# Down product as three products of split operands, scatters with a bounds check and a value projection that starts at the first tile, in a two-layer convolution, attention and mixture-of-experts trunk

## The reference

```
scores = sigmoid(xt @ router_w)                    # 64 experts, the 8 best of each token
h = silu(xb @ w_gate[e]) * (xb @ w_up[e])          # xb: an expert's tokens, up to 128 a block; 1024 -> 256
y = h @ w_down[e]                                  # 256 -> 1024, times the token's gate
routed[token] += y                                 # over the 8 experts of each token
out = routed + shared expert
```

## Time and profile before

| | us |
|---|---|
| median of the 3 runs (lowest, highest) | 2486.3 (2479.9, 2489.4) |
| the profiled execution, its own time | 2482.5 |
| its span, first to last instruction | 2480.7 |
| TensorE busy | 2296.2 |
| VectorE busy | 1606.8 |
| ScalarE busy | 1076.4 |
| GpSimd busy | 684.8 |

### The profile page before, as it was taken

One profiled execution on the slowest core, in us unless ns is written; L12 is line 12 of the kernel. 1 busy time (PEld: TensorE's weight loads), 2 busy tenths in 40 slices (PEclk: granted clock), 3 DMA queues, 4 the chain that ended last, 5 costly groups with the idle time before them and its releaser, 6 DMA issues.

```text
span 2480.7 us, 32934 instructions
## 1 busy us (share of the span) xinstructions
PE 2296.2 (93%) x9437; PEld 1633.7 (66%) x9437; DVE 1606.8 (65%) x1737; ACT 1076.4 (43%) x1215; POOL 684.8 (28%) x698
## 2 busy tenths in 40 slices
PE   7948889999999999869999999798999999999994
PEld 4413557767666667559988888554667777676673
DVE  4874557777767667552377787436677777776675
ACT  3651135555555555422243333112555555555552
POOL 3970213443434333200000000002233433334331
PEclk9969889999999999979999999889999999999997
DMA  6210359999999999633322222132999999999994
GB/s 216 68 34 0 127 202 346 371 366 375 360 350 362 365 345 372 209 134 93 94 77 69 79 83 83 56 119 70 339 366 367 368 364 363 367 372 355 360 364 142
DMA packets 197117, 592.57 MB, mean 239 GB/s; under 512 B 26605, under 2 KB 96277, under 8 KB 161732
## 3 DMA queue, kind: packets, MB, share of 16 engines
q1 hardware_dynamic: 165140, 517.92, 56.0%
q0 software_dynamic: 31920, 73.91, 12.2%
HBM read 579.16 MB, written 51.38 MB: 254 GB/s over the span
## 4 chain that ended last, share of the span: by engine, by line
PE 81%; DVE 6%; DMA 4%; ACT 1%; issue 1%; POOLq 0%; SPq 0%; DVEq 0%; ACTq 0%
PE PS L1355 29%; PE PS L1376 18%; PE PS L1464 11%; PE PS L1448 5%; PE PS L1246 5%; PE PS L1342 5%; DMA W<-in_exp_w_down 4%; PE PS L1280 2%; PE PS L1477 1%; PE PS L1364 1%; PE PS L1502 1%; PE PS L1326 1%; DMA acc<-BIG,IDXS 1%; PE PS L1299 1%; PE PS L1489 1%
## 5 line engine op out<-in xcount | busy, mean ns | idle before, releaser
L998 DVE TENSOR_TENSOR WL<-W,WH 128x2048 fp32r<-128x2048 f32 x276 | 621.3, 2293 | 197.3 <-ACT WH L679 185.9
L679 ACT ACTIVATE WH<-W 128x2048 fp32r<-128x2048 f32 x276 | 512.4, 1907 | 43.1 <-DVE IDX L976 42.4
L1376 PE MATMUL PS<-W,BIG 128*128 128x512 f32 x1104 | 498.6, 594 | 11.1 <-issue 5.0
L1355 PE MATMUL PS<-WH,XH 128*128 128x512 f32 x1104 | 446.6, 405 | 8.8 <-DVE XL L991 8.8
L1355 PE MATMUL PS<-WH,XL 128*128 128x512 f32 x1104 | 435.2, 394 | 0.0
L1355 PE MATMUL PS<-WL,XH 128*128 128x512 f32 x1104 | 432.6, 392 | 0.0
L589 POOL DMA_INDIRECT acc<-BIG,IDXS x138 | 259.1, 1878 | 471.3 <-issue 371.3
L1376 PEld LDWEIGHTS PS<-W,BIG 128*128 128x128 f32 x1104 | 199.2, 190 | 212.8 <-issue 205.1
L1355 PEld LDWEIGHTS PS<-WH,XH 128*128 128x128 f32 x1104 | 209.7, 190 | 48.2 <-DVE XL L991 9.6
L689 ACT ACTIVATE BIG<-PS 128x512 f32<-128x512 f32 x138 | 82.5, 598 | 362.5 <-PE PS L1376 362.5
L1355 PEld LDWEIGHTS PS<-WH,XL 128*128 128x128 f32 x1104 | 209.2, 189 | 46.0
(11 more groups left out here) (233 smaller groups left out, 3110.2 us busy)
## 6 DMA issues: line engine op xcount, KB each, us to landing
W<-in_exp_w_gate SPq DMA_DIRECT2D x138, 1024.0 KB
W<-in_exp_w_up SPq DMA_DIRECT2D x138, 1024.0 KB
W<-in_exp_w_down SPq DMA_DIRECT2D x138, 1024.0 KB
RAW<-in_w_kv SPq DMA_DIRECT2D x48, 512.0 KB, 3.8
RAW<-in_attn_w_q SPq DMA_DIRECT2D x24, 512.0 KB, 3.7
W<-in_conv_w_in SPq DMA_DIRECT2D x8, 1024.0 KB, 11.4
acc<-BIG SPq DMA_DIRECT2D x9, 512.0 KB, 3.7
W<-in_conv_w_out SPq DMA_DIRECT2D x4, 1024.0 KB, 6.5
```

Source lines behind the costliest of these rows:

```text
L679: A(WH[:, s, c, :], W[:, 3 - 3 * s + c, :], ACT.Copy).then_inc(s_wh[l], 1)
L998: v.tensor_tensor(WL[s][:, c, :], W[:, 3 - 3 * s + c, :], WH[:, s, c, :].bitcast(F32), ALU.subtract).then_inc(s_wl[l], 1)
L1355: last = mm(PS[:, 3 + s, :].rearrange("p (a b) -> p a b", a=2), a, w, start=(k == 0 and i == 0), stop=(k == KT - 1 and i == 2))
L1376: last = mm(PS[:, 5 + h, :], HTm[:, s, k * P:(k + 1) * P], wd[:, k, h * 512:(h + 1) * 512], start=(k == 0), stop=(k == 1))
```

## The change

The down product becomes a split product like gate/up's. ScalarE copies the down weights to a high part `WDH` and the transposed hidden to `HTH`; VectorE subtracts to get `WDL` and `HTL`; TensorE sums three products, 12 matmuls of 512 columns in float32r. Both halves of the output are now copied by ScalarE. The loads of gate and up wait for a count of low parts that now has the down parts in it; the load of down waits as before. The scatter has a bounds check at row 511, and the spare rows of `acc`, with the store of zeros to them at the start, are gone. Gathers stay four blocks ahead. Between the layers, three pieces of `w_kv` are split ahead of the norm instead of two behind it, and the V product of the first three pieces runs tile by tile as the tiles come; only from the fourth piece on it runs over all tiles. The next norm's vectors are loaded behind piece 9 instead of piece 3. Left out of the diff are hunks that only merge the semaphores `s_pj` and `s_tb` of the two layers into one each.

```diff
--- before.py
+++ after.py
@@ -45,7 +45,7 @@
     xrows = nc.dram_tensor("xrows", [T, D], F32, kind="Internal").ap()
-    acc = nc.dram_tensor("acc", [T + P, D], F32, kind="Internal").ap()
+    acc = nc.dram_tensor("acc", [T, D], F32, kind="Internal").ap()
     etab = nc.dram_tensor("etab", [2, OVER], I32, kind="Internal").ap()
@@ -130,6 +130,13 @@
+        _, WDH1, HTL, _, HTH, WDH0, _, WDL = lay_out([("to_WDH1", [8192 + 10240], F32), ("WDH1", [2, D], F32R), ("HTL", [2, F], F32R),
+                                                      ("to_HTH", [20736 - 12800], F32), ("HTH", [2, F], F32R),
+                                                      ("WDH0", [2, D], F32R), ("to_WDL", [256], F32),
+                                                      ("WDL", [SLOTS, CH], F32R)])
+        WDH = (WDH0, WDH1)
+
+
         _, XTH, _, RAW, PH, PL, XTL = lay_out([("to_XTH", [NT, D], F32), ("XTH", [KT, T], F32R), ("to_RAW", [23552], F32),
@@ -184,10 +191,9 @@
         Hm = big(20224, 2, F)
-        HTm = big(20736, 2, F)
-
-
-        s_vec, s_posd, s_zero = sem("vec_loaded"), sem("pos_loaded"), sem("zeros_stored")
+
+
+        s_vec, s_posd = sem("vec_loaded"), sem("pos_loaded")
         s_xin = [sem(f"x_loaded{n}") for n in range(NT)]
@@ -238,10 +244,10 @@
         s_ht = [sem(f"hidden_transposed{i}") for i in range(2)]
-        s_he = [sem(f"hidden_T_copied{i}") for i in range(2)]
+        s_hh = [sem(f"hidden_T_high{i}") for i in range(2)]
+        s_he = [sem(f"hidden_T_low{i}") for i in range(2)]
         s_yd = [sem(f"expert_out{i}") for i in range(2)]
-        s_ya = [sem(f"expert_out_low_copied{i}") for i in range(2)]
-        s_yv = [sem(f"expert_out_high_copied{i}") for i in range(2)]
+        s_ya = [sem(f"expert_out_copied{i}") for i in range(2)]
         s_scat = [sem(f"scattered{i}") for i in range(2)]
@@ -389,7 +395,7 @@
                     for c in range(2):
-                        sp.wait_ge(s_wl[l], b * 2 - 3 + c)
+                        sp.wait_ge(s_wl[l], 1 + c if isinstance(b, int) and b == 2 else b * 3 - 6 + c)
                         load(3 - 3 * s + c, e)
@@ -429,8 +435,6 @@
                 sp.dma_start(RB[:, l, :], router_bias[l:l + 1, :].broadcast_to([P, E])).then_inc(s_rw, 16)
-            sp.wait_ge(s_cst, 1)
-            sp.dma_start(acc[T:T + P, :], XG[:, 0, :]).then_inc(s_zero, 16)
             for i in range(6, n_first):
@@ -438,7 +442,7 @@
             for j, src in enumerate(pieces):
-                if j == PIECES:
+                if j == 3 * PIECES:
                     ln_vectors(2)
@@ -462,7 +466,6 @@
             sp.wait_ge(s_out, 16 * NT)
-            sp.wait_ge(s_zero, 16)
@@ -474,7 +477,6 @@
-            pool.memset(XG[:, 0, :], 0.0)
             pool.memset(ones[:, :], 1.0)
@@ -524,7 +526,6 @@
                 pool.wait_ge(s_norm, 2 * NT * l + NT)
-                pool.wait_ge(s_zero, 16)
                 link(pool.memset(XG[:, 0:2, :], 0.0))
@@ -579,15 +580,14 @@
                     pool.wait_ge(s_ic[l], copies)
-                    pool.wait_ge(s_ya[l], b + 1)
-                    pool.wait_ge(s_yv[l], b + 1)
+                    pool.wait_ge(s_ya[l], b * 2 + 2)
                     if not (isinstance(b, int) and b == 0):
 ...
                         pool.indirect_dma_start(acc, bass.IndirectOffsetOnAxis(IDXS[0:r, s:s + 1], axis=0), YB[0:r, s, :],
-                                                None, compute_op=ALU.add).then_inc(s_scat[l], 16)
+                                                None, bounds_check=T - 1, oob_is_err=False, compute_op=ALU.add).then_inc(s_scat[l], 16)
@@ -678,24 +678,40 @@
+                def down_high(b, s, it):
+                    act.wait_ge(s_mw[l][5 - 3 * s], it * 16 + 16)
+                    if not (isinstance(b, int) and b < 2):
+                        act.wait_ge(s_yd[l], b - 1)
+                    A(WDH[s].rearrange("p k n -> p (k n)"), W[:, 5 - 3 * s, :], ACT.Copy).then_inc(s_wh[l], 1)
+
+                def hidden_high(b, s):
+                    act.wait_ge(s_ht[l], b + 1)
+                    if not (isinstance(b, int) and b < 2):
+                        act.wait_ge(s_yd[l], b - 1)
+                    A(HTH[:, s, :], PS[:, 2, 0:F], ACT.Copy).then_inc(s_hh[l], 1)
+
                 def silu(b, s):
 ...
-                def out_low(b, s):
+                def out(b, s):
                     act.wait_ge(s_yd[l], b + 1)
 ...
                         act.wait_ge(s_scat[l], (b - 1) * 16)
-                    A(YB[:, s, 0:512], PS[:, 5, :], ACT.Copy).then_inc(s_ya[l], 1)
+                    for h in range(2):
+                        A(YB[:, s, h * 512:(h + 1) * 512], PS[:, 5 + h, :], ACT.Copy).then_inc(s_ya[l], 1)
                 def step(b, s, it, more):
+                    hidden_high(b, s)
                     if more:
 ...
                         rows_high(b + 2, s)
-                    out_low(b, s)
+                    if more or s == 0:
+                        down_high(b + 1, 1 - s, it + s)
+                    out(b, s)
@@ -714,13 +730,16 @@
                 rows_high(1, 1)
+                down_high(0, 0, 0)
+                for k in range(2):
+                    act.wait_ge(s_acc[l][k], 16 * NT // 2)
                 step(0, 0, 0, True)
 ...
                     step(it * 2 + 1, 1, it, True)
-                step(n * 2 - 2, 0, None, False)
-                step(n * 2 - 1, 1, None, False)
+                step(n * 2 - 2, 0, n - 1, False)
+                step(n * 2 - 1, 1, n - 1, False)
@@ -767,7 +786,6 @@
             moe(0)
-            norm_round(1)
@@ -778,10 +796,12 @@
-            for j in range(PIECES - 1):
+            for j in range(PIECES):
                 piece_high(j)
+            norm_round(1)
             for j in range(n_v):
-                piece_high(j + PIECES - 1)
+                if j >= 1:
+                    piece_high(j + PIECES - 1)
                 if j % 4 == 3:
@@ -994,7 +1014,7 @@
                     for c in range(2):
-                        dve.wait_ge(s_wh[l], b * 2 + 1 + c)
+                        dve.wait_ge(s_wh[l], b * 2 + 1 + c if isinstance(b, int) and b < 2 else b * 3 + c)
                         v.tensor_tensor(WL[s][:, c, :], W[:, 3 - 3 * s + c, :], WH[:, s, c, :].bitcast(F32),
@@ -1005,25 +1025,25 @@
-                def hidden_T(b, s):
-                    dve.wait_ge(s_ht[l], b + 1)
-                    v.tensor_copy(HTm[:, s, :], PS[:, 2, 0:F]).then_inc(s_he[l], 1)
-
-                def out_high(b, s):
-                    dve.wait_ge(s_yd[l], b + 1)
-                    if not (isinstance(b, int) and b < 2):
-                        dve.wait_ge(s_scat[l], (b - 1) * 16)
-                    v.tensor_copy(YB[:, s, 512:D], PS[:, 6, :]).then_inc(s_yv[l], 1)
+                def down_low(b, s, copies):
+                    dve.wait_ge(s_wh[l], copies)
+                    v.tensor_tensor(WDL[:, 5 - 3 * s, :], W[:, 5 - 3 * s, :],
+                                    WDH[s].rearrange("p k n -> p (k n)").bitcast(F32), ALU.subtract).then_inc(s_wl[l], 1)
+
+                def hidden_low(b, s):
+                    dve.wait_ge(s_hh[l], b + 1)
+                    v.tensor_tensor(HTL[:, s, :], PS[:, 2, 0:F], HTH[:, s, :].bitcast(F32), ALU.subtract).then_inc(s_he[l], 1)
                 def step(b, s, more):
-                    hidden_T(b, s)
+                    hidden_low(b, s)
                     if more:
 ...
                         rows_low(b + 2, s)
-                    out_high(b, s)
+                    if more or s == 0:
+                        down_low(b + 1, 1 - s, b * 3 + 8 if more else n * 6)
@@ -1035,6 +1055,7 @@
                 rows_low(1, 1)
+                down_low(0, 0, 5)
                 step(0, 0, True)
@@ -1118,10 +1138,12 @@
-            for j in range(PIECES - 1):
+            for j in range(PIECES):
                 piece_low(j)
+            norm_round(1)
             for j in range(n_v):
-                piece_low(j + PIECES - 1)
+                if j >= 1:
+                    piece_low(j + PIECES - 1)
                 if j % 4 == 3:
@@ -1345,7 +1367,7 @@
                     pe.wait_ge(s_xl[l], b + 1)
-                    pe.wait_ge(s_wl[l], b * 2 + 2)
+                    pe.wait_ge(s_wl[l], b * 2 + 2 if isinstance(b, int) and b < 2 else b * 3 + 1)
                     if not (isinstance(b, int) and b < 2):
@@ -1364,17 +1386,19 @@
-                def down_proj(b, s, it):
+                def down_proj(b, s, splits):
                     pe.wait_ge(s_he[l], b + 1)
-                    pe.wait_ge(s_mw[l][5 - 3 * s], it * 16 + 16)
+                    pe.wait_ge(s_wl[l], splits)
                     if not (isinstance(b, int) and b == 0):
-                        pe.wait_ge(s_ya[l], b)
-                        pe.wait_ge(s_yv[l], b)
-                    wd = W[:, 5 - 3 * s, :].rearrange("p (k n) -> p k n", k=2)
+                        pe.wait_ge(s_ya[l], b * 2)
+                    wdl = WDL[:, 5 - 3 * s, :].rearrange("p (k n) -> p k n", k=2)
```

(59 more changed lines are left out.)

2 lines of the change are left out of this document (1 added, 1 removed).

## The result

The changed kernel takes **2569.31 us** (median of 4 runs, 2565.21 to 2571.77); the kernel before took 2484.99 in the same rounds. The ratio is 1.0339, 95% interval [1.0321, 1.0357]: slower by 84 us, outside the predicted range. The profiled execution has a span of 2566.1 us, 85.4 more than before.

A forecast was written before the change was run, and what follows sets the result against it. It took TensorE's program and the full DMA engines as joint bounds; 5 + 3 - 5 = +3 us on the profiled 2482.5 gave 2485.5, and 2489 us as the median. The range was 2445 to 2535 us.

The forecast's parts named there:

- the slower rival: Expert blocks: down weights land late, ScalarE's copy waits in front of its program; 10.4 us per block, 2525 us, chance 0.16.
- the new order on ScalarE: Expert blocks: next block's down copy stands ahead of output and later copies; two-block loop, 10.15 us per block, +5 us.
- Landing to issue, 10.3: Two-block loop: from down weights' landing through ScalarE's and VectorE's copies and SyncE's issues to next down issue, 10.3 us.
- The landing, 9.6: Two-block loop: down transfer from issue to landing, 2.5 + 9.8 - 2.7 = 9.6 us.
- The spread, 0.2: Expert blocks: allowance for uneven scatters, twice today's 0.11 us, added to 9.95 us per block.
- TensorE's idle time: Expert blocks: the 0.7 us saved on TensorE goes into waiting for VectorE's low copies; 0.6 to 0.9 us idle per block.
- Faster, DMA-bound at 9.8: Expert blocks: less queued DMA serves transfers quicker, blocks of 9.8 to 9.85 us, -38 us, 2446 us; chance 0.34.
- Scatters: Expert blocks: scatters wait for each other, GpSimd slowed by VectorE subtractions; loop grows 0.3 us, +40 us, 2529; chance 0.09.
- No saving: Scatters: bounds check leaves padded rows' cost, DMA time stays 10.07, block 10.3 us, 2510 us; chance 0.06.
- the signs named: Expert blocks: signs of being right, with blocks 10.1 to 10.2 us apart; 9.8 or below, or above 10.3, meant wrong.
- The V product: Value projection between layers: tile-by-tile start beside a norm about 11 us later, -5 us, between -13 and +5.
- The start and end of the stages, +3: Each expert stage: copies ahead of the first step and one more serial hop at the end, +1.5 us per layer.

The follow-up runs named there:

- e6: Changed kernel with SyncE loading the down weights' expert number ahead of its waits for the gate and up slots: 2569.49 us, ratio 1.0331.
- e11: Changed kernel with the up loads behind the first ones bringing only half their bytes: 2460.57 us (one run).
- e4: Changed kernel with SyncE issuing the down load ahead of gate and up instead of behind them: 2487.74 us, ratio 1.0036.
- e2: Kernel before with the scatters' bounds check alone: 2481.3 us, ratio 0.9991.
- e1: Kernel before with the split down product alone, no bounds check, V product as before: 2584.55 us, ratio 1.0415.
- e10: Changed kernel with loads in the order down, gate, up and both expert numbers loaded ahead of the waits: 2502.79 us, ratio 1.0075.
- e12: Changed kernel with the down weights' high and low copies moved into their own block's step and loads ordered down, gate, up: 2545.59 us (one run).
- e3: Changed kernel with down weights loaded only for the first two blocks of a layer: 2418.2 us (one run).

## Why the prediction was wrong

*The mechanism was one of its rivals, mispriced.* The late landing was there as the slower rival, 2525 us at a chance of 0.16. The step that failed is the sum of **the new order on ScalarE**: 10.3 (landing to next issue) + 9.6 (landing), with 0.2 of spread, 10.15 us per block. The trace has 10.8 + 11.2 in the chain (mean of 43 landings), 11.0 per block where the loop holds, and 10.82 on average: 0.67 us per block more, 132 times, 88 us (+5 was said for the blocks, +93.5 came); the other terms took some 6 us off again.

- *Landing to issue, 10.3, was 10.8.* I let down's issue follow the low copies by 0.5 us. It also has up's issue ahead of it and the load of its own expert number (the row of L402 and what surrounds it): up is issued at 1969.02, down at 1970.28, 1.26 behind. The steps were all in the trace of before; the number's load was not counted. The copies ahead of it came 0.3 us shorter than summed (up's issue 9.5 us behind the landing, 9.8 said), which hides a part of that miss. e6 shows that this term alone could be had back without any gain.
- *The landing, 9.6, was the larger error.* I took it as the mean work of the queue, 9.8 us a block from gate's issue on plus 2.5. Gate's issue to down's landing was to be 12.3 and is 14.1 in the median: two of the three loads and the rows stand ahead of down, and it has landed only when the slowest of the 16 engines has (the first is done 7.4 us behind the issue, the last 10.5, medians). e11 shows which way this depends: half a megabyte less ahead of it, 1.9 us sooner. e6 shows the other side: an issue 0.6 us sooner, nothing. So the form, a drain of what is queued from gate's issue on, had the right direction and was 1.8 us too small. A landing of fixed length behind its own issue, my first reading of the result, was wrong. How the 1.8 us divide between the spread of the engines and dearer bytes stays open.
- *The spread, 0.2, has no measure of its own.* The chain's landings run from 9.4 to 13.7 us; it is part of the difference between the median 10.5 and the chain's mean of 11.2.
- *A term that was not there: the clock.* TensorE's idle time was forecast, 0.6 to 0.9 us per block, and taken as harmless. The slow gate/up products behind it are 18 us of the chain, up to a fifth of the 93.5; their cause is still the late landing, as e4 has 5 of them and not 18. What the time would be with the waits and the full clock, no run shows.
- *The rival's own sum.* (10.3 + 10.5) / 2 is 10.4 without the 0.2 of spread that the forecast adds. With it the rival is 10.6, about +65 us, some 2550, outside the stated range.
- *The other rivals.* "Faster, DMA-bound at 9.8" had the wrong floor. It rests on the time that the skipped rows save, and in e2 the weights' queue took 14 of the 35 us back; the 368 GB/s beside it is the figure of one window. Over 400 to 1000 and 1850 to 2400 us the kernel before moves 363 and 364 GB/s at a share of 1.01, e2 358 and 359 at 1.00 and 1.01, e4 358 and 357 at 0.99 and 0.98. So with the bounds check the engines stayed as full and moved 1% less, and no run with all the weights has blocks below the 10.11 us of the kernel before. The Trainium skill (DMA: Bandwidth & Descriptors, Specifications) gives about 358 GB/s as the HBM limit and 368 derated; over these stretches the kernel before lies between the two, and e2 and e4 at the first. Whether a version without any loop would get below 10.2 no run shows; in e4 the last load of the three, now up, is again in the chain. "Scatters" is out as first cause, by e1 and e4: GpSimd waits less for an earlier scatter than before, 354 us against 390.7, though stretches of the chain run through them (4% of the span), and in e10 and e12 they hold 15%. The contention that the Trainium skill names (GPSIMD Engine Reference, Key points) does not set the pace here: in e4 the gathers' index copy takes 1152 ns in the mean, in the changed kernel 882, and e4 is 82 us faster. Only in e3, with 1821 ns, does GpSimd hold much of the chain. "No saving" is out for the second queue, with 67.18 MB and 10.5% as worked out, but not for the blocks: e2 shows the engines as full as before.
- *What held.* The split product takes 2.76 us per block (2.74 to 3.0 said; the row of L1401 at 2078.78 above).

ScalarE waiting for the landing before its new copy, the share just under 1 and 0.6 to 0.9 us of idle TensorE per block (7.9 in 100 us, 0.85) were the signs named; all three came, and so did the 67 MB of the second queue. They fit the slower rival as well, so they told nothing of which was right; what did tell was the distance of the blocks, 10.8 us, above the 10.3 named as a sign of being wrong. The V product came near in number, and in part by luck: the norm starts 14.1 us behind the last scatter's landing (3.4 before), 10.7 later where 11 was said, the first V product stands inside it, and the stage from the last block on takes 1259.71 - 1077.98 = 181.7 us against 187.2, -5.5 for a predicted -5. Of these, 3.6 lie between the last scatter's landing and the end of the V product (162.9 us against 166.5); the other 1.9 lie ahead of that landing, where the forecast had put 0 to +4.

```profile
1094.31 2.46 DMA acc<-BIG,IDXS
...
1110.88 1.29 DVE bns L904 x2
...
1122.20 5.98 PE PS L1463 x18
...
1259.71 0.46 PE PS L1502 x2
```

The start and end of the stages, +3, came as about 0 at the start and the end of the execution and as these -1.9 between the layers. The stretch between V product and layer 1 is 2.7 us shorter, for which the forecast had no term and I have no cause: 93.5 - 5.5 - 2.7 = 85.3 of the span's 85.4.

## What to carry to other kernels

A copy that moves ahead of other work on an in-order engine turns a hidden transfer into a loop: then count, from the trace, every issue and register load up to the next issue, and price the landing as the drain of everything queued before it, until the slowest engine is done, not as its bytes and a latency. Give the last place in the queue to the load that is needed last; here that order alone was worth 82 us. Count on no idle time of TensorE as free: here slow-clock products came behind it. And before moving a copy later, add up the new two-block path of the compute engines: it may be as long as the one it removes.

## What the runs showed of the hardware

- In both orders a 1 MB load landed later, the later it was issued among the three. The down weights landed 10.5 us after their issue in the median as the last (changed kernel) and 8.2 as the first (e4, same bytes), where up, now the last, took 12.8 (e4's page):

```profile
W<-in_exp_w_gate SPq DMA_DIRECT2D x138, 1024.0 KB, 9.8
W<-in_exp_w_up SPq DMA_DIRECT2D x138, 1024.0 KB, 12.8
W<-in_exp_w_down SPq DMA_DIRECT2D x138, 1024.0 KB, 8.2
```

- In the kernel before the same load landed 14.5 us after its issue in the median and cost some 14 us in all, at 368 GB/s in the window. In the changed kernel gate, up and down landed after 6.9, 9.0 and 10.5 us, at 334 GB/s. A shorter landing was the sign of a queue with pauses, not of a better one.
- The rate fell by 9% (368 to 334 GB/s) while the DMA share fell by 5% (1.02 to 0.97): in this window a byte took 5% longer as well. Over the whole span the weights' queue took 3% more time for the same bytes (55.8% of 2566.1 us against 56.0% of 2480.7). Read GB/s beside the share.
- In the expert blocks of the changed kernel TensorE's granted clock fell to 1.2 GHz behind some of its pauses, 16 times for 3.4 us and twice for 6.8. A gate/up product that met this took 7.1 to 8.5 us and not 5.7; the changed kernel has 18 such products, e12 and the kernel before none.
